# State-space stage of a two-layer hybrid block: tiles ordered by tables, head steps spread into the next group, three projection banks, normalisation moved into attention

## Chip, core and metric

The kernel runs on one core of one Trainium2 chip. A core has five engines that run their own instruction streams side by side and wait for each other by semaphores: TensorE (PE, matrix products into the eight PSUM banks `ps0` to `ps7`; the profile shows its weight loads as PEld), VectorE (DVE), ScalarE (ACT), GpSimd (POOL) and SyncE (SP, which here issues the transfers). The metric is the device time of one execution in microseconds (us), the median of three runs. The output has to agree with the reference.

## What is computed

Two layers of a first block are followed by two layers of a second one. The change touches only the first block, and in it the state-space branch. Cut to what matters (`x` is 256 tokens by 1024; 32 heads of width 64 in 4 groups of 8; state 128):

```python
for layer in range(2):
    proj = einsum('bsd,de->bse', x, w_in[layer])       # z 2048, xbc 3072, dt 64, attention inputs, gates 3072
    xbc = silu(centred_dwconv(xbc, conv_w, conv_b))    # 5 taps along the tokens
    xs, bm, cm = split(xbc)                            # 2048, 4 groups x 128, 4 groups x 128
    dt = softplus(dt_raw + dt_bias)                    # 2 directions x 32 heads
    # both directions: y[q] += sum_s (cm[q].bm[s]) * exp(cum[q] - cum[s]) * dt[s] * xs[s]
    y = y_fwd + y_bwd + d_skip * xs
    y = y * silu(z)
    y_ssd = rmsnorm(y, norm_w)                         # over all 2048 channels
    # differential attention, memory cross attention, gates
    merged = g0 * (y_ssd @ w_br_ssd) + g1 * (y_diff @ w_br_diff) + g2 * (y_cross @ w_br_cross)
    x = layernorm(ALPHA * x + merged @ w_out)
```

## The kernel before

**Weights and tiles.** Every product with a weight matrix is made in tiles of 128 output columns by 256 tokens. All are fp32, split in two: SyncE loads a unit of 256 weight columns (two tiles, 512 KB) into one of two `raw` buffers (L367); ScalarE copies a tile of it to `w_hi` (`split`, L956); VectorE makes `w_lo = raw - w_hi` (`split`, L1389); TensorE makes a tile with 24 matmuls, three for each of 8 slices (`proj` and `passes`, L498 to L500). There are four tile places in `w_hi` and `w_lo`, so TensorE may be at most four tiles behind the splits. A `raw` buffer is loaded again when both engines have split both its tiles. Each engine works in the order in which its code is written.

**State-space stage.** Each group has 16 tiles: x0 to x3, b, c (convolution inputs), z0 to z3, and six gate tiles. Their results go to two banks, `ps0` and `ps1`, by turns. ScalarE takes a tile out of its bank. A convolution tile is copied to `conv_in` and gets its first tap from ScalarE (`first_tap`), four taps from VectorE (`conv`, L1596, one `SCALAR_TENSOR_TENSOR` each), a tanh from ScalarE and its product from VectorE (`conv_silu`, L1601). When all six are through, TensorE transposes x (L655), multiplies b by c (L660), and VectorE makes `x_dt` (L1630) and the masked `cb` (L1635 to L1638). Then come the eight heads: TensorE spreads a row of cumulated decay over 128 partitions (`spread_rows`, L668), ScalarE makes the decay (`decays`, four Relu pieces and an Exp, L953), VectorE weighs it with `cb` (`weigh`, L1643), TensorE multiplies two heads at a time (`head_pair`, L681), VectorE adds the skip and applies z (`gate_y`, L1648 and L1651), ScalarE squares, GpSimd sums. The last seven tiles of the group are written between the head steps, and the heads end with the group.

**Start of a layer.** TensorE makes tiles 0 to 2 (`first_three`) and `dt_tiles` (L619 to L621). VectorE works `dt_softplus` (L1563 to L1582) behind the fourth convolution tile. `cumulate` (L630 to L637) waits for it, and the head steps wait for `row_ready`, which VectorE gives at L1623.

**Behind the stage.** TensorE sums the squares (`square_sum`, L698), VectorE makes 1/(mean + eps), ScalarE the root, and VectorE scales the 16 tiles of `y_ssd` (L1671) before it goes on to the splits of the first attention step. In attention (4 steps of 20 tiles) `token_tile` (L712 to L714) needs two of these splits at once. The branch stage begins with ScalarE's and VectorE's split of all `y` tiles (`y_hi`, `y_lo` at L1748); ScalarE waits for `ssd_ready` before the first and for `att_ready` before the third.

## Time and profile before

| | |
|---|---|
| runs, us | 2633.53, 2632.78, 2635.39 (median 2633.53) |
| the profiled execution, us | 2640.17 |
| its span (first to last instruction), us | 2638.4 |
| mean granted TensorE clock | 0.983 |
| TensorE matmul / weight load busy | 94% / 89% |
| VectorE / ScalarE busy | 65% / 51% |
| read from memory | 372.31 MB, 142 GB/s |

The state-space stage runs from about 51 to 318 us in layer 0 and from 703 to 977 us in layer 1; the attention steps follow. A row of the timeline gives the start, the time, the engine, the line and what is written and read, and in brackets how long the engine was idle before it and what ended that. Times of neighbouring instructions overlap a little, so that a cost is best read from one start to the next. Of a matmul the end is modelled; starts are what to go by.

### The profile page before, as it was taken

To read this page: it belongs to the slowest core of one execution; us is meant where nothing else is said; L and a number is where in the kernel's file an instruction comes from. 1 tells how busy PE (TensorE), PEld (TensorE's weight loads), DVE (VectorE), ACT (ScalarE), POOL (GpSimd) and SP (SyncE) were. 2 spreads that over 40 slices of the span, in tenths; PEclk is the share of its full clock that TensorE was granted. 3 is DMA by queue.
4 is the path that set the end of the run, shared out by engine and by line. 5 is a ranking of instruction groups with operands and counts; after the bars stand their busy time and mean duration, and the time that the engine had idled before them with its cause. 6 is when DMAs were issued, how large, how long until landed. Compare 5 with 4: busy or idle time off the path is not lost.

```text
span 2638.4 us, 51861 instructions
## 1 busy us (share of the span) xinstructions
PE 2470.2 (94%) x18994; PEld 2352.6 (89%) x18994; DVE 1725.0 (65%) x2597; ACT 1349.5 (51%) x2368; POOL 88.9 (3%) x96
## 2 busy tenths in 40 slices
PE   5888899999978889999999999999999999989998
PEld 4788799999978879999999998789999999779998
DVE  4677766765767776676576566567656656557655
ACT  4677644553567764555344444534445444544443
POOL 0000000000000000000010010001001001001000
PEclk9999999999989999999999999999999999999999
DMA  5344444435334444443545544234554554423553
GB/s 153 112 129 129 128 131 156 138 123 186 114 112 129 129 128 135 153 143 122 183 151 180 171 149 146 84 128 159 175 171 151 173 175 147 124 89 123 181 173 109
DMA packets 386828, 375.60 MB, mean 142 GB/s; under 512 B 14894, under 2 KB 385502, under 8 KB 386542
## 3 DMA queue, kind: packets, MB, share of 16 engines
q1 hardware_dynamic: 386670, 373.41, 44.9%
q8 instruction: 109, 1.79, 0.3%
q14 instruction: 49, 0.40, 0.0%
HBM read 372.31 MB, written 1.05 MB: 142 GB/s over the span
## 4 chain that ended last, share of the span: by engine, by line
PE 65%; issue 24%; DVE 5%; ACT 3%; POOLq 1%; DVEq 1%; DMA 1%; POOL 0%; SPq 0%; ACTq 0%
PE ps L498 18%; PE ps L500 18%; PE ps L499 18%; PE ps L712 1%; POOLq L463 1%; ACT w_hi L956 1%; PE ps L713 1%; PE ps L714 1%; DVE w_lo L1389 1%; PE ps L738 1%; PE ps L484 1%; DVE xT L1495 1%; PE ps L726 1%; PE ps L769 1%; PE ps L759 1%
## 5 line engine op out<-in xcount | busy, mean ns | idle before, releaser
L1389 DVE TENSOR_TENSOR w_lo<-raw,w_hi 128x1024 fp32r<-128x1024 f32 x704 | 860.6, 1229 | 441.7 <-ACT w_hi L956 439.5
L498 PE MATMUL ps<-x_hi,w_hi 128*128 128x272 f32 (+1 forms) x3648 | 1062.4, 291 | 24.1 <-DVE w_lo L1389 16.6
L499 PE MATMUL ps<-x_lo,w_hi 128*128 128x272 f32 (+1 forms) x3648 | 1043.2, 286 | 0.0
L500 PE MATMUL ps<-x_hi,w_lo 128*128 128x272 f32 (+1 forms) x3648 | 1042.0, 286 | 0.0
L956 ACT ACTIVATE w_hi<-raw 128x1024 fp32r<-128x1024 f32 x704 | 736.1, 1054 | 538.6 <-PE ps L500 378.0
L498 PEld LDWEIGHTS ps<-x_hi,w_hi 128*128 128x128 f32 x3648 | 690.5, 189 | 55.0 <-issue 27.6
L499 PEld LDWEIGHTS ps<-x_lo,w_hi 128*128 128x128 f32 x3648 | 692.0, 190 | 2.4
L500 PEld LDWEIGHTS ps<-x_hi,w_lo 128*128 128x128 f32 x3648 | 692.2, 190 | 0.0
L498 PE MATMUL ps<-big_r,w_hi 128*128 128x272 f32 x832 | 244.6, 294 | 12.3 <-DVE scratch L1934 8.6
L500 PE MATMUL ps<-big_r,w_lo 128*128 128x272 f32 x832 | 242.8, 292 | 0.0
L956 ACT ACTIVATE scratch<-ps 128x256 f32<-128x256 f32 (+7 forms) x312 | 115.5, 384 | 184.9 <-PE ps L714 89.8
L499 PE MATMUL ps<-gates_r,w_hi 128*128 128x272 f32 x704 | 202.4, 288 | 0.0
L499 PE MATMUL ps<-big_r,w_hi 128*128 128x256 f32 (+1 forms) x640 | 185.5, 290 | 0.0
L498 PEld LDWEIGHTS ps<-big_r,w_hi 128*128 128x128 f32 x832 | 159.3, 191 | 14.6 <-issue 14.2
L500 PEld LDWEIGHTS ps<-big_r,w_lo 128*128 128x128 f32 x832 | 159.4, 192 | 0.0
L953 ACT ACTIVATE scratch<-ps 128x272 f32<-128x272 f32 (+2 forms) x168 | 66.8, 400 | 180.1 <-PE ps L500 164.5
L498 PE MATMUL ps<-scratch_r,w_hi 128*128 128x256 f32 x512 | 146.6, 286 | 4.4 <-DVE big_r L1748 4.4
L500 PE MATMUL ps<-scratch_r,w_lo 128*128 128x256 f32 x512 | 145.7, 285 | 0.0
L499 PEld LDWEIGHTS ps<-gates_r,w_hi 128*128 128x128 f32 x704 | 132.7, 189 | 0.2
L1596 DVE SCALAR_TENSOR_TENSOR scratch<-scratch,pa_all 128x256 f32<-128x256 f32 x192 | 92.9, 484 | 53.1 <-ACT scratch L953 28.7
L499 PEld LDWEIGHTS ps<-big_r,w_hi 128*128 128x128 f32 x640 | 125.3, 196 | 0.0
L453 POOL TENSOR_TENSOR xT<-xT,norm_bias 128x272 f32<-128x272 f32 (+1 forms) x56 | 51.5, 952 | 1786.1 <-DVE x_lo L1503 1786.1
(287 smaller groups left out, 3102.8 us busy)
## 6 DMA issues: line engine op xcount, KB each, us to landing
raw<-in_w_in SPq DMA_DIRECT2D x224, 512.0 KB, 4.7
raw<-in_ffn_w_up SPq DMA_DIRECT2D x176, 512.0 KB, 4.3
raw<-in_ffn_w_down SPq DMA_DIRECT2D x64, 512.0 KB, 4.3
raw<-in_mix_w_in SPq DMA_DIRECT2D x64, 512.0 KB, 4.6
raw<-in_w_mem_kv SPq DMA_DIRECT2D x32, 512.0 KB, 4.3
raw<-in_w_br_ssd SPq DMA_DIRECT2D x32, 512.0 KB, 4.3
raw<-in_ffn_w_down SPq DMA_DIRECT2D x32, 384.0 KB, 3.5
raw<-in_w_br_diff SPq DMA_DIRECT2D x16, 512.0 KB, 4.0
```

The lines of the kernel that those rows point to most:

```text
L453: m = pool.tensor_tensor(x, x, norm_bias[:, o:o + 1].to_broadcast([P, n]), ALU.add)
L463: pool.drain()
L484: m = mm(out, w, x, start=(j == 0), stop=(j == n - 1))
L498: mm(out, wh, xh, start=first, stop=False)
L499: mm(out, wh, xl, start=False, stop=False)
L500: return mm(out, wl, xh, start=False, stop=last)
L712: mm(out, xh, wh, start=(j == 0), stop=False)
L713: mm(out, xh, wl, start=False, stop=False)
L953: return act.activation(out, in_, f, **kw)
L956: return act.activation(out, in_, ACT.Copy, scale=scale)
L1389: tt(w_lo[:, p % PARTS, :, :], raw[:, p // 2 % RAW, :, (p % 2) * P:(p % 2 + 1) * P], wh_f[:, p % PARTS, :, :], ALU.subtract).then_inc(lo_r ...
L1596: m = stt(c, conv_in[:, j, n:n + SEQ], tap(n), c, ALU.mult, ALU.add)
```

## The change

- The group loop of SyncE and the attention loops of ScalarE and VectorE are written out instead of looped. The order of the 16 tiles of a group, and the place (the tile number) behind which each head step stands, come from tables. A place of 16 or more lies in the next group (or, for the last group, in the first attention step).
- Projection tiles take three banks (`ps0`, `ps1`, `ps5`) in turn; TensorE waits for the tile three back to be taken out. Sum of squares and `cb` move to `ps7`.
- ScalarE takes the middle tap straight from the bank and `conv` makes the taps 0, 1, 3, 4. `decays` writes the Relu pieces straight to `decay`, so it waits for `y_done` before them. The z tiles no longer share a buffer with the convolution.
- The row of `row_ready` is made by VectorE at place 8 of group 0, behind five convolution tiles, and TensorE waits for it before tile 9.
- The norm: TensorE sums the squares behind tile 7 of attention step 0, ScalarE takes the root behind the root of that step, VectorE inverts at its end and scales 6, 5 and 5 tiles in steps 1, 2 and 3. `ssd_ready` is given at the end of step 3.

```diff
+CONV_ORDER = ("b", "c", "x0", "x1", "x2", "x3")
+FIRST_GROUP = ("g0", "g1", "z0", "z1", "b", "c", "x0", "x1", "x2", "x3", "g2", "g3", "z2", "z3", "g4", "g5")
+NEXT_GROUP = ("b", "c", "x0", "x1", "g0", "g1", "x2", "x3", "z0", "z1", "g2", "g3", "z2", "z3", "g4", "g5")
+SPREAD_AT = later((9, 10, 11, 12, 15, 16, 17, 18), (3, 4, 6, 7, 13, 14, 15, 16))
+DECAY_AT = later((10, 11, 12, 13, 16, 17, 18, 19), (4, 5, 8, 9, 14, 15, 16, 17))
+WEIGH_AT = later((11, 12, 13, 14, 17, 18, 19, 20), (7, 8, 10, 11, 15, 16, 17, 18))
+PAIR_AT = later((15, 16, 19, 21), (13, 14, 17, 19))
+GATE_AT = later((16, 17, 20, 22), (14, 15, 18, 20))
+CB_AT, MASK_AT = later(9, 5), later(10, 6)
+XS_AT, XDT_AT = later(13, 11), later(14, 12)
+NORM_TILES = ((), range(0, 6), range(6, 11), range(11, 16))
...
 # TensorE
+                    for k in range(16):
+                        n = g * 16 + k
+                        if n >= 3:
+                            pe.wait_ge(gf[(n - 3) % 2], LH + A_H + (n - 3) // 2 + 2)
+                            proj(Q, T, k, k, x1, own=banks[(n + 1) % 3])
+                        if n == 6:
+                            cumulate()
+                        if n == 8:
+                            pe.wait_ge(S["cum_ready"], l + 1)
+                            pe.wait_ge(S["row_ready"], l + 1)
+                            pe.wait_ge(S["rows_cleared"], l + 1)
+                        if g:
+                            heads(g - 1, k + 16)
+                        heads(g, k)
...
 # VectorE
+                    for k in range(16):
+                        if MASK_AT[g] == k:
+                            mask_cb(g)
+                        if XDT_AT[g] == k:
+                            x_by_dt(g)
+                        if tiles[k] in CONV_ORDER:
+                            conv(CONV_ORDER.index(tiles[k]), k)
+                        if g == 0 and k == 2:
+                            dt_exponent()
+                        split(Q, k + 4)
+                        if tiles[k][0] == "z":
+                            z_silu_tile(int(tiles[k][1]), k)
+                        if k >= 3 and tiles[k - 3] in CONV_ORDER:
+                            conv_silu(CONV_ORDER.index(tiles[k - 3]))
+                        if g == 0 and k == 3:
+                            dt_softplus()
+                        if g == 0 and k == 8:
...
+                        if g:
+                            heads(g - 1, k + 16)
+                        heads(g, k)
...
-                v.wait_ge(S["ssq_done"], l + 1)
-                ts(rs_ssd[:, 0, :], ps[5][:, 0:SEQ], 1.0 / SSD_INNER, NORM_EPS, ALU.mult, ALU.add)
-                v.drain()
-                v.reciprocal(rs_ssd[:, 1, :], rs_ssd[:, 0, :]).then_inc(S["ssd_var"], 1)
...
+                    for j in NORM_TILES[i]:
+                        norm_y(j)
...
+                    if i == 0:
+                        v.wait_ge(S["ssd_rs"], l + 1)
+                        v.reciprocal(rs_ssd[:, 0, :], rs_ssd[:, 1, :])
+                    if i == 3:
+                        v.drain()
+                        v.sem_inc(S["ssd_ready"], 1)
```

Three places where instructions move, all on VectorE, each with the semaphores waited for. First, the start of a layer. Before, `dt_softplus` (from `waits dt_exp`) stands behind convolution taps:

```order
L1596 SCALAR_TENSOR_TENSOR scratch<-scratch,pa_all 128x256
L1596 ISA
L1596 SCALAR_TENSOR_TENSOR scratch<-scratch,pa_all 128x256
L1388 REGISTER_ALU
L1389 TENSOR_TENSOR w_lo<-raw,w_hi 128x1024 [waits weights_hi_ready]
L1601 SCALAR_TENSOR_TENSOR scratch<-scratch 128x256 [waits conv_tanh]
L1561 REGISTER_ALU
L1563 TENSOR_SCALAR big<-big 128x128 [waits dt_exp]
```

After, it stands behind two splits and the two z tiles (`bank_free`), and no tap has been made yet:

```order
L1630 SCALAR_TENSOR_TENSOR big<-big 128x128
L1461 REGISTER_ALU
L1462 TENSOR_TENSOR w_lo<-raw,w_hi 128x1024 [waits weights_hi_ready]
L1442 ISA
L1727 SCALAR_TENSOR_TENSOR scratch<-scratch 128x256 [waits bank_free0]
L1461 REGISTER_ALU
L1462 TENSOR_TENSOR w_lo<-raw,w_hi 128x1024 [waits weights_hi_ready]
L1727 SCALAR_TENSOR_TENSOR scratch<-scratch 128x256 [waits bank_free1]
L1634 REGISTER_ALU
L1636 TENSOR_SCALAR big<-big 128x128 [waits dt_exp]
```

Five convolution tiles now stand between the softplus and the row for `row_ready`, where before there were two.

Second, a head of a middle group. Before, `weigh` (L1643) stands between a split and `gate_y`, with no taps near:

```order
L1389 TENSOR_TENSOR w_lo<-raw,w_hi 128x1024
L1642 REGISTER_ALU
L1643 TENSOR_TENSOR big<-big,scratch 128x768
L1388 REGISTER_ALU
L1389 TENSOR_TENSOR w_lo<-raw,w_hi 128x1024
L1648 ISA
L1648 SCALAR_TENSOR_TENSOR scratch<-scratch,skip,ps 128x256
L1651 SCALAR_TENSOR_TENSOR big<-scratch 128x256
```

After, places 16 to 18 of a group: each `weigh` (now L1682) stands behind the four taps (L1714) and the split of a convolution tile of the next group:

```order
L1714 SCALAR_TENSOR_TENSOR scratch<-scratch,pa_all 128x256
L1461 REGISTER_ALU
L1462 TENSOR_TENSOR w_lo<-raw,w_hi 128x1024 [waits weights_hi_ready]
L1681 REGISTER_ALU
L1682 TENSOR_TENSOR big<-big,scratch 128x768 [waits decay_ready]
L1442 REGISTER_ALU
L1714 ISA [waits bank_free0]
L1714 SCALAR_TENSOR_TENSOR scratch<-scratch,pa_all 128x256
```

The head pair that waits for this `weigh` now waits for those taps as well.

Third, the entry of attention. Before, the norm (a loop of four times four `L1671`) stands ahead of the first splits:

```order
L1664 TENSOR_SCALAR scratch<-ps 128x256 [waits ssq_done]
L1666 RECIPROCAL scratch<-scratch 128x256
L1667 UNCONDITIONAL_BRANCH
L1671 ISA [waits ssd_rs]
L1671 ISA
L1671 SCALAR_TENSOR_TENSOR big<-big,pb_all,scratch 128x256
```

After, the splits of attention step 0 stand between the last three `weigh` and two `gate_y` of the last group:

```order
L1462 TENSOR_TENSOR w_lo<-raw,w_hi 128x1024 [waits weights_hi_ready]
L1681 REGISTER_ALU
L1682 TENSOR_TENSOR big<-big,scratch 128x768 [waits decay_ready]
L1461 REGISTER_ALU
L1462 TENSOR_TENSOR w_lo<-raw,w_hi 128x1024 [waits weights_hi_ready]
L1681 REGISTER_ALU
L1682 TENSOR_TENSOR big<-big,scratch 128x768 [waits decay_ready]
L1688 ISA [waits y_done]
```

The norm is gone from here, and with it the wait for `ssq_done`.

## Rows read from the trace of the kernel before

**Rows 1.** The page, section 1: engine, busy us (share), instructions.

```profile
PE 2470.2 (94%) x18994; PEld 2352.6 (89%) x18994; DVE 1725.0 (65%) x2597; ACT 1349.5 (51%) x2368; POOL 88.9 (3%) x96
```

**Rows 2.** Waits of PE, whole run: who waited, for whom, total us, times, longest.

```profile
PE ps L681 <- DVE big L1643: 22.0, 14, 2.7
PE ps L498 <- DVE w_lo L1389: 16.6, 11, 6.9
PE ps L655 <- issue: 11.4, 2, 5.8
...
PE ps L712 <- DVE w_lo L1389: 6.5, 2, 3.3
```

**Rows 3.** Windows: one group in each layer, then attention entry (stretch, length, busy, PEclk).

```profile
218.00:282.20 64.20, 56.64 (x469) 52.68 (x469) 47.84 (x75) 46.29 (x94) 4.49 (x4) 1.00 0.44 132
875.30:941.10 65.80, 58.34 (x469) 53.91 (x469) 47.93 (x75) 46.27 (x94) 4.49 (x4) 0.97 0.42 129
318.30:346.10 27.80, 22.69 (x156) 21.71 (x155) 19.13 (x35) 8.02 (x13) 1.46 (x2) 0.88 0.36 114
```

**Rows 4.** Timeline of PE: a tile starts, a spread row and a pair, the next tile.

```profile
98.66 0.28 PE L498 MATMUL ps<-x_hi,w_hi 128*128 128x256 f32 x1
...
101.50 0.40 PE L668 MATMUL ps<-cum_rows,head_sel 128*128 128x512 f32 x1
...
103.28 0.38 PE L498 MATMUL ps<-x_hi,w_hi 128*128 128x256 f32 x1
```

**Rows 5.** Timeline of DVE: a convolution tile, its split, a product; a later split.

```profile
208.63 0.48 DVE L1596 SCALAR_TENSOR_TENSOR scratch<-scratch,pa_all 128x256 f32<-128x256 f32 x1
...
210.99 1.22 DVE L1389 TENSOR_TENSOR w_lo<-raw,w_hi 128x1024 fp32r<-128x1024 f32 x1
212.12 0.42 DVE L1601 SCALAR_TENSOR_TENSOR scratch<-scratch 128x256 f32<-128x256 f32 x1
...
214.82 1.22 DVE L1389 TENSOR_TENSOR w_lo<-raw,w_hi 128x1024 fp32r<-128x1024 f32 x1
```

**Rows 6.** Timeline of DVE: x_dt (cb follows), a weigh; then a gate_y.

```profile
224.32 2.48 DVE L1630 TENSOR_TENSOR scratch<-ps,dt_tok 128x512 f32<-128x512 f32 x4
...
228.02 0.96 DVE L1643 TENSOR_TENSOR big<-big,scratch 128x768 f32<-128x768 f32 x1 [0.16 <-issue]
...
237.93 0.48 DVE L1648 SCALAR_TENSOR_TENSOR scratch<-scratch,skip,ps 128x256 f32<-128x256 f32 x1 [0.21 <-issue]
...
238.83 0.95 DVE L1643 TENSOR_TENSOR big<-big,scratch 128x768 f32<-128x768 f32 x1
```

**Rows 7.** Timeline of ACT: a split that waited for its transfer, then a head's decay and the next.

```profile
221.76 1.06 ACT L956 ACTIVATE w_hi<-raw 128x1024 fp32r<-128x1024 f32 x1 [4.31 <-DMA raw<-in_w_in]
222.72 1.34 ACT L953 ACTIVATE scratch<-ps,cum_tok 128x256 f32<-128x256 f32 x4
...
224.89 1.33 ACT L953 ACTIVATE scratch<-ps,cum_tok 128x256 f32<-128x256 f32 x4
```

**Rows 8.** Timeline of DVE, layer 1: softplus's first, the tap behind it, the row.

```profile
724.22 0.22 DVE L1563 TENSOR_SCALAR big<-big 128x128 f32<-128x128 f32 x1
...
730.38 0.48 DVE L1596 SCALAR_TENSOR_TENSOR scratch<-scratch,pa_all 128x256 f32<-128x256 f32 x1
...
746.19 0.68 DVE L1623 TENSOR_TENSOR cum_rows<-ps,cum_rows 32x512 fp32r<-32x512 f32 x1
```

**Rows 9.** Attention entry: the norm on DVE, ahead of the splits.

```profile
326.79 6.42 DVE L1671 SCALAR_TENSOR_TENSOR big<-big,pb_all,scratch 128x256 f32 x16 [0.81 <-ACT scratch L953]
```

**Rows 10.** Start of the branch stage: ACT's first copies, DVE's first `y_lo`.

```profile
562.33 1.99 ACT L956 ACTIVATE scratch_r<-big 128x1024 fp32r<-128x1024 f32 x2
...
565.20 6.90 DVE L1748 TENSOR_TENSOR big_r<-big,scratch_r 128x1024 fp32r<-128x1024 f32 x6 [0.18 <-issue]
```

**Rows 11.** Windows in which the granted clock was at its lower level.

```profile
335.00:341.80 6.80, 5.74 (x26) 5.65 (x27) 3.28 (x3) 0.21 (x1) 0.00 (x0) 0.50 0.69 226
823.10:826.50 3.40, 3.40 (x18) 2.95 (x15) 3.08 (x5) 2.66 (x6) 0.00 (x0) 0.50 0.53 138
```

More of the change, by code:

```diff
@@ L73 @@
 K_EPS = K_INV + 1
-K_SUB = K_EPS + 2
+K_SUB = K_EPS + 3
 K_COLS = K_SUB + P
@@ new lines, in heads @@
+                def heads(g, at):
+                    for j in range(HEADS_PER_GROUP):
+                        if SPREAD_AT[g][j] == at:
+                            spread_rows(g, j)
+                    for p in range(4):
+                        if PAIR_AT[g][p] == at:
+                            head_pair(g, p)
+                    if XS_AT[g] == at:
+                        turn_x(g)
+                    if CB_AT[g] == at:
+                        b_by_c(g)
+                banks = (ps[0], ps[1], ps[5])
@@ new lines, in square_y, with heads @@
+                def square_y(g, p):
+                    n = g * 4 + p
+                    act.wait_ge(S["y_gated"], l * 16 + n + 1)
+                    if n >= 2:
+                        act.wait_ge(S["sq_added"], l * 16 + n - 1)
+                    fn(y_sq[:, p % 2, :], y_ssd[:, n, :], ACT.Square).then_inc(S["y_squared"], 1)
+                def heads(g, at):
+                    for j in range(HEADS_PER_GROUP):
+                        if DECAY_AT[g][j] == at:
+                            decays(g, j)
+                    for p in range(4):
+                        if SQUARE_AT[g][p] == at:
+                            square_y(g, p)
@@ L1056, in _ @@
-                    copy(conv_in[:, :, 0:2], zeros)
-                    copy(conv_in[:, :, 2 + SEQ:4 + SEQ], zeros)
-                    for j in range(6):
-                        done(T, j)
-                        bank = {2: ps[6], 3: ps[5]}.get(j, ps[j % 2]) if g == 0 else ps[j % 2]
-                        copy(conv_in[:, j, 2:2 + SEQ], bank[:, 0:SEQ]).then_inc(gf[j % 2], 1)
-                        act.drain()
-                        first = g * 4 + j if j < 4 else g + 16 + 4 * (j - 4)
-                        fn(xbc[:, j, :], conv_in[:, j, 0:SEQ], ACT.Identity, scale=taps[:, ds(l * PA_ROWS + first, 1)],
-                           bias=pb_[:, ds(l * PB_ROWS + first + PB_CONVB, 1)]).then_inc(S["first_tap"], 1)
-                        split(Q, j + 4)
-                        if j:
-                            conv_tanh(j - 1)
-                        if g == 0 and j == 2:
+                    tiles = GROUP_TILES[g]
@@ new lines, in conv_first @@
+                    def conv_first(c, k, b):
+                        if g and c >= 2:
+                            act.wait_ge(S["y_gated"], G * 4 + c - 5)
+                        first = g * 4 + c - 2 if c >= 2 else g + 16 + 4 * c
+                        out = x_c[:, c - 2, :] if c >= 2 else bc[:, c, :]
+                        fn(out, b, ACT.Identity, scale=taps[:, ds(l * PA_ROWS + first + 2 * CONV_TILES, 1)],
+                           bias=pb_[:, ds(l * PB_ROWS + first + PB_CONVB, 1)])
+                        copy(conv_in[:, c, 2:2 + SEQ], b).then_inc(gf[k % 2], 1)
@@ new lines, in _ @@
+                    if g == 0:
+                        zeros = view(const, K_CAUS2, 6, 2)
+                        copy(conv_in[:, :, 0:2], zeros)
+                        copy(conv_in[:, :, 2 + SEQ:4 + SEQ], zeros)
+                        for k in range(3):
+                            evac_tile(k)
+                    for k in range(16):
+                        if g or k >= 3:
+                            evac_tile(k)
+                        split(Q, k + 4)
+                        if k >= 2 and tiles[k - 2] in CONV_ORDER:
+                            conv_tanh(CONV_ORDER.index(tiles[k - 2]))
+                        if g == 0 and k == 2:
@@ L1134, in _ @@
+                        if g:
+                            heads(g - 1, k + 16)
+                        heads(g, k)
+                for i in range(4):
                     Q, T, N = L + i * 4 + B_Q, LH + i * 8 + B_H, l * 4 + i
@@ L1676, in _, with norm_y @@
+                def norm_y(j):
+                    y = y_ssd[:, j, :]
+                    stt(y, y, pb_[:, ds(l * PB_ROWS + (PB_NORM + j), 1)], rs_ssd[:, 0, :], ALU.mult, ALU.mult)
+                for i in range(4):
                     Q, T, N = L + i * 4 + B_Q, LH + i * 8 + B_H, l * 4 + i
```

387 lines of the change are left out of this document (187 added, 200 removed).

## Prediction

> **What bounds the kernel now.** I read the page first: TensorE is busy 94% of the span and VectorE 65% [rows 1], so time is lost only where TensorE waits. The list of its waits says for whom: nearly all of the long ones end with VectorE's work (`weigh` at L1643, `w_lo` at L1389), and the wait at L655 is the start of a layer [rows 2]. The windows then tell where. A group in the middle of the state-space stage takes 64.2 us in layer 0, of which TensorE is busy 56.6 and VectorE 47.8, and 65.8 in layer 1, where the granted clock has also been at its lower level (1.2 instead of 2.4 GHz) for one stretch; the entry of attention takes 27.8 us with 22.7 busy [rows 3]. So about 7.6 us in each middle group, 5 at each attention entry and some 10 to 14 at each layer start are waits. All this is some 90 us, half of it within the groups.
>
> **Prices.** TensorE: a tile 98.66 to 101.50 = 2.84; spread row and pair together 1.78, of which I give the row 0.34 [rows 4]. VectorE: four taps 2.36, a split 1.13, a product with the tanh about 0.34 (0.42 less the overlap) [rows 5]; `x_dt` and masked `cb` together 3.7, `weigh` 0.88 (0.96 less the overlap), `gate_y` 1.1 with the idle ahead of it [rows 6]. ScalarE: split 0.96, a head's decay 2.17 [rows 7]; taking out a tile 0.3 to 0.8. A transfer into a `raw` buffer is usable 5.7 us after VectorE's last split of it: the one that starts at 214.82 ends at 216.0 [rows 5], and ScalarE's split that waits for the transfer starts at 221.76 [rows 7]. The work of TensorE stays the same but for its place. So the sum is one of waits, and I worked a timetable, place for place, each engine in its new order, with these prices.
>
> **The start of a layer.** Before, `row_ready` comes at 746.9 in layer 1 [rows 8]. After, VectorE sits idle until z1 is out of its bank (about 717.9, since tile 3 ends behind the dt tiles), works the softplus of 724.22 to 730.38 = 6.2 [rows 8] until 724.1, and then five convolution tiles with splits (5 x 3.5), two products and the row: 18.9, so `row_ready` comes at 743.0. TensorE has done tile 8 at 732.5 and waits 10.5 in one piece for it, where before it waited 6.9 for a `w_lo` and 5.8 for the row [rows 2]. Behind it the transposes wait 1.3 for the product of x3. Counting what head work is still owed at the end of the group's 16 tiles, layer 1 gains 3.6 us; in layer 0, where ScalarE was not late before, the same timetable gives 0.1. Sum **-4**.
>
> **Groups 1 to 3.** In places 0 to 2 VectorE now makes four taps, a split, and behind them a `weigh` or `gate_y` of the group before: 4.4 to 5.5 us a place, against 2.84 to 4.6 on TensorE. The pair at place 17 needs the `weigh` of place 16, which comes 5.7 us after tile 0 is done, while TensorE is there after 3.2: wait 2.5. The pair at 19 waits 2.4 in the same way. Then the transposes at place 11 wait for the product of x3, which stands behind split 14. That split waits for a transfer released by split 11, behind x3's own taps: 5.7 + 0.96 + 1.13 + 0.34 = 8.2 us after it, wait 2.3. Group 1 is worse, because group 0's tables are later by two places: 4.3, 0.5 and 3.4. In all 22.6 by starts (about 20.8 as the windows count idle), against three times 7.6: a gain of 2.0 a layer, 4 in both. So the waits do not leave the groups, they change their place. The clock of before fell once within a group in layer 0 and three times in layer 1 (823.10 is one of them) at some 1.6 each [rows 11]: 6.5 comes back if it stays up. Sum **-10.5** before what the clock does after the change.
>
> **Attention entry.** The norm (6.4 us of VectorE [rows 9] ahead of four splits) goes, and with it the wait of `token_tile`, the wait for the square sum and the lower clock from 335.0 to 341.8 [rows 11]. The stretch of 27.8 [rows 3] holds 19.0 of work at full clock (four tiles, two token tiles of 2.9, 1.8 for the rotation); the pairs moved into it are owed by the groups. VectorE has only 1.13 + 0.88 a place here, so its pairs wait 0.4 each. 0.35 of the square sum is only moved. 27.8 - 19.0 - 0.8 - 0.35 = 7.65 a layer: **-15.3**. This is the surest term.
>
> **The norm's new place.** 16 products of 0.40 [rows 9] in three steps stand on VectorE ahead of a split that ScalarE had ready some 4 us before TensorE needs it, and 1.75 for the inversion stands ahead of splits which end 1.3 us before their token tile: zero. If the cover were gone, the queue behind them (splits 4 and 5 of step 1) would cost at most 1.75 a layer. ScalarE's root costs nothing, it stands next to another root.
>
> **The branch stage.** `ssd_ready` now comes at the end of step 3. ScalarE's first two copies, at 562.33, move behind VectorE's last product: the first `y_lo`, at 565.20 [rows 10], comes when one copy is through, 1.05 later. Sum **+2.1**.
>
> **Loops written out.** TensorE waits for nothing at the loop ends of attention, so 0; bounds: -2 and +4, the latter from the idle of some 2.6 that ScalarE shows once around a table load at the start of layer 1.
>
> **The clock after the change.** Sum so far: -4 - 10.5 - 15.3 + 2.1 = -27.7. Eight waits of over 2 us are left in groups 1 to 3 of a layer, 16 in all. The rows show both outcomes of such waits: after the 2.7 us at a head pair [rows 2] the clock stayed up in two of three groups of layer 0 (1.00 in rows 3), in layer 1 it fell each time, for 3.4 us at 0.50 (823.10), and around the 3.3 us at the token tile [rows 2] it was down for 6.8 (335.00) [rows 11]. A fall costs half of what of it is worked: 1.7 or 2.9. For the two long waits of group 1 I take 2.3 each, for the six others every second time 1.7: 9.7 a layer, of which about a fifth falls into the next wait anyway. That is +16. The Trainium skill ("TensorE: Matmul & The Clock Gate", section "Why this matters for your kernels") warns of idle gaps between bursts of matmuls, since the clock then drops. By that rule, with which the falls in the trace agree, splitting the waits into more pieces does not help unless each gets short; taken strictly it gives the slower rival below.
>
> **Sum.** -27.7 + 16 = -11.7. From the profiled execution, 2640.2, this is 2628.5; the runs' median lies 6.6 lower at 2633.5, so I forecast **2622**.
>
> **Rivals.**
> 1. *The clock stays up.* All 16 waits pass without a fall, since TensorE works at least two tiles between them. For it speaks layer 0, against it layer 1. -27.7: **2606**. If VectorE also lags less than by my timetable (its sum of 52 us a group fits under 56), the three waits of a group shrink by 1 us each, 18 more: 2588 is the far end.
> 2. *The clock falls after every one of the 16 waits and takes 6.8 us to come back*, as it did at 335.00 [rows 11]: 16 x 2.9 = 46 against 27.7: +18, **2652**, slower. It decides from 27.7 / 16 = 1.7 us a wait on. Against it: waits of 2.7 us so far cost 1.6 or nothing.
> 3. *Gain and loss cancel.* ScalarE now has decays, tanh and two passes of a convolution tile in one place (2.2 + 0.3 + 0.8 + 0.96 = 4.3 against 2.84), so a split reaches VectorE late, and what VectorE does late meets TensorE as a longer wait. 2 us more in each of six groups is 12: **2633.5**, no change.
> 4. *The change doesn't take effect*: the norm is in fact gone from the entry by the order of instructions, so this could only hold for the groups, and there it is my forecast that they gain 2 us a layer.
>
> **How the numbers follow.** Forecast 0.48, rival 1 0.17, rival 2 0.18, rival 3 0.17. The measurement tells some 0.2%, 5.3 us, from no change. Faster: forecast and rival 1, less the forecast's own upper tail, 0.62; the same 0.16; slower 0.22. The forecast's own range is 2610 to 2630. The range of 8 in 10 takes in most of rival 1 and rival 2 short of its last third: 2601 to 2646.
>
> **What would show it.** In the changed profile: one wait of about 10.5 us of TensorE for the row at the start of each layer; per group, waits of about 2.5, 2.4 and 2.3 us for `weigh`, `weigh` and a product of the convolution, longer in group 1; an attention entry with no wait over 1 us and a full clock; the branch stage's first wait 1 us longer than before. Middle groups of 63 us at full clock would be the forecast, under 60 rival 1's far end, over 65 rival 2 or 3, told apart by the granted clock. The forecast is wrong if VectorE's places 0 to 3 take other than 4.4 to 5.5 us, or if the transfer is not what gates x3's product.

## The result, and the profile after

The changed kernel takes **2667.5 us** (median of 4 runs, 2665.4 to 2672.0) against 2633.2 us for the kernel before (4 runs, 2629.3 to 2635.4): ratio 1.0131, 95% interval 1.0119 to 1.0143. It is slower by 34 us, where I had forecast 2622 us and a range that ended at 2646. The profiled execution took 2672.0 us with a span of 2670.2, which is 31.8 us more than the span of before.

The page of the changed kernel, section 1, answers to [rows 1]: engine, busy us, share of the span, instructions.

```profile
PE 2483.3 (93%) x18994; PEld 2365.7 (89%) x18994; DVE 1730.0 (65%) x2595; ACT 1335.5 (50%) x2354; POOL 82.1 (3%) x96
```

TensorE has the same 18994 matmuls and is 13 us longer busy with them. More matmul time for the same matmuls goes with a lower clock: the mean granted clock of the profiled execution is 0.973, where it was 0.983. The list of TensorE's waits answers to [rows 2] (who waited, for whom, total us, times, longest). L703 is the head pair (L681 before), L673 the transposes of x (L655 before), L524 the first matmul of a projection tile (L498 before):

```profile
PE ps L703 <- DVE big L1682: 44.7, 16, 5.5
PE ps L673 <- DVE scratch L1722: 26.2, 8, 5.3
PE ps L524 <- issue: 20.5, 2, 10.3
```

The pairs' waits for `weigh` have doubled, from 22.0 to 44.7 us. A wait of 26.2 us for the product with the tanh (`conv_silu`) has taken the place of 11.4 us in which the transposes waited at the layer starts. The two waits of 10.3 are the row at the start of a layer, and they are as long as forecast. The long waits for `w_lo` inside the stage and the wait at the token tile (L712 before) are gone. ("issue" stands where the profile shows no engine that TensorE waited for.)

Windows of the changed kernel, from the first matmul of a group's first tile to that of the next group's: group 1, 2 and 3 of layer 0, the same of layer 1, then the stretch from attention's first tile to the rotation in each layer. Columns: stretch, length, busy (instructions) of PE, PEld, DVE, ACT and POOL, granted clock, DMA share, GB/s. The rows for group 2 and the entry answer to [rows 3]. Group 1 has 5.3 us of group 0's head steps in it.

```profile
119.00:193.20 74.20, 62.40 (x488) 57.33 (x487) 50.20 (x77) 45.40 (x95) 3.44 (x4) 0.91 0.38 114
193.20:262.50 69.30, 59.51 (x469) 55.39 (x468) 49.29 (x74) 44.88 (x92) 3.60 (x4) 0.95 0.40 122
262.50:334.00 71.50, 60.77 (x469) 56.39 (x468) 49.30 (x74) 44.91 (x92) 3.60 (x4) 0.93 0.38 119
790.70:865.50 74.80, 62.79 (x488) 57.67 (x487) 50.23 (x77) 45.45 (x95) 3.44 (x4) 0.91 0.37 113
865.50:935.10 69.60, 59.45 (x470) 55.34 (x469) 49.30 (x74) 44.91 (x92) 3.60 (x4) 0.95 0.40 122
935.10:1009.10 74.00, 62.80 (x470) 57.92 (x468) 49.29 (x74) 44.91 (x92) 3.60 (x4) 0.88 0.37 115
334.00:354.00 20.00, 17.97 (x154) 16.52 (x153) 12.50 (x15) 13.83 (x28) 2.67 (x3) 1.00 0.36 114
1009.10:1029.10 20.00, 17.97 (x155) 16.55 (x154) 12.50 (x15) 13.83 (x28) 2.68 (x3) 1.00 0.37 117
```

A group takes 69 to 75 us where it took 64 to 66, the granted clock is at 0.88 to 0.95 instead of 1.00 or 0.97, and VectorE is busy for 49 of the 70. It is not short of time over a group as a whole. The entry of attention is the one place that went as planned: full clock and hardly a wait.

Cut at the first matmuls of the same tiles, both layers together, the 31.8 us are these. In the second line the work that the change moves over a border is put back to where it was: 5.3 us a layer of head steps from group 0 into group 1, and 3.2 us a layer from group 3 into attention (three pairs and three spread rows, then two pairs and one row; a row 0.34, a pair 1.44, [rows 4]).

| Stretch | layer start and group 0 | groups 1 to 3 | entry to the rotation | steps of attention | branch stage to next start | the rest |
|---|---|---|---|---|---|---|
| after less before, us | -11.1 | +42.4 | -6.1 | +0.2 | +4.1 | +2.3 |
| moved work put back | -0.5 | +38.2 | -12.5 | +0.2 | +4.1 | +2.3 |
| forecast | -4 | +5.5 (-10.5 +16) | -15.3 | 0 | +2.1 | 0 |

So 32.7 of the 43.5 us between the forecast for the profiled execution (2628.5) and what it took lie in groups 1 to 3.

**One wait, read out.** Four timelines of the changed kernel around the pair of place 17 in layer 0 (start, us, engine, line, what, and in brackets the idle time ahead with what ended it). TensorE first: the last matmul of tile 0, then the pair.

```profile
265.24 0.27 PE L526 MATMUL ps<-x_hi,w_lo 128*128 128x256 f32 x1
...
272.62 2.81 PE L703 MATMUL ps<-big,scratch 128*64 128x256 f32 x16 [3.97 <-DVE big L1682]
```

ScalarE, which takes tile 0 out at L1001 and L1004 (266.39 and 266.84):

```profile
263.90 1.35 ACT L1001 ACTIVATE big<-ps,cum_tok 128x256 f32<-128x256 f32 x4
265.33 0.85 ACT L1001 ACTIVATE big<-big 128x768 f32<-128x768 f32 x1
266.08 0.40 ACT L1001 ACTIVATE y_sq<-big 128x256 f32<-128x256 f32 x1
266.39 0.55 ACT L1001 ACTIVATE scratch<-ps,pb_all,pa_all 128x256 f32<-128x256 f32 x1
266.84 0.37 ACT L1004 ACTIVATE scratch<-ps 128x256 f32<-128x256 f32 x1
```

VectorE and, in the last row, GpSimd: a `weigh`, the two instructions of the gating, the first tap of tile 0, its split, the `weigh` that releases the pair, and GpSimd's addition to the sum of squares.

```profile
265.18 0.95 DVE L1682 TENSOR_TENSOR big<-big,scratch 128x768 f32<-128x768 f32 x1
266.35 0.48 DVE L1688 SCALAR_TENSOR_TENSOR scratch<-scratch,skip,ps 128x256 f32<-128x256 f32 x1 [0.21 <-issue]
266.90 0.68 DVE L1691 SCALAR_TENSOR_TENSOR big<-scratch 128x256 f32<-128x256 f32 x1
267.50 0.47 DVE L1714 SCALAR_TENSOR_TENSOR scratch<-scratch,pa_all 128x256 f32<-128x256 f32 x1
...
269.86 1.22 DVE L1462 TENSOR_TENSOR w_lo<-raw,w_hi 128x1024 fp32r<-128x1024 f32 x1
271.00 1.48 DVE L1682 TENSOR_TENSOR big<-big,scratch 128x768 f32<-128x768 f32 x1
...
270.70 0.96 POOL L491 TENSOR_TENSOR y_sum<-y_sum,y_sq 128x256 f32<-128x256 f32 x1 [3.41 <-ACT y_sq L1001]
```

My timetable had this `weigh` ready 5.7 us after tile 0 was done, and it took 7.0 (265.5 to 272.48). Two things were missing in it. When tile 0 ends, ScalarE still has place 15's decay and square to do, and VectorE the `weigh` and the gating of place 15 (until 267.58). ScalarE has tile 0 out at 267.21, so of the two it is VectorE's own queue that ends last. So the first tap starts 2.0 us after the tile, where my 5.7 leaves 1.3 once four taps, a split and a `weigh` are taken off. And the `weigh` takes 1.48 us where I had 0.88. These 1.3 us make up most of the 1.8 between the wait forecast (2.5, from start to start) and the gap measured (4.26); most of the rest is that TensorE was there 2.9 us after tile 0 and not 3.2.

### The profile page after: what moved, and what is told of

The parts are those of the page before. It is cut to its first block, busy times and chain, and to the rows that moved or that the text cites. A ratio compares the mean times of both kernels' runs of the same rounds, so it can differ in the third digit from the quotient of the medians.

```text
span 2670.2 us, 51795 instructions
## 1 busy us (share of the span) xinstructions
PE 2483.3 (93%) x18994; PEld 2365.7 (89%) x18994; DVE 1730.0 (65%) x2595; ACT 1335.5 (50%) x2354; POOL 82.1 (3%) x96
## 3 DMA queue, kind: packets, MB, share of 16 engines
HBM read 372.31 MB, written 1.05 MB: 140 GB/s over the span
## 4 chain that ended last, share of the span: by engine, by line
PE 76%; DVE 9%; ACT 5%; issue 3%; DVEq 3%; DMA 3%; ACTq 1%; SPq 0%
PE ps L524 20%; PE ps L526 20%; PE ps L525 20%; ACT w_hi L1004 2%; DVE w_lo L1462 2%; PE ps L703 2%; DVE scratch L1714 1%; PE ps L757 1%; PE ps L758 1%; PE ps L759 1%; ACT big L1001 1%; DVEq L1686 1%; DMA raw<-in_w_in 1%; ACTq L1106 1%; ACT scratch L1004 1%
## 5 line engine op out<-in xcount | busy, mean ns | idle before, releaser
L524 PE MATMUL ps<-x_hi,w_hi 128*128 128x272 f32 (+1 forms) x3648 | 1066.2, 292 | 28.9 <-issue 20.5
L1004 ACT ACTIVATE w_hi<-raw 128x1024 fp32r<-128x1024 f32 x704 | 736.4, 1055 | 493.0 <-PE ps L526 375.6
L524 PEld LDWEIGHTS ps<-x_hi,w_hi 128*128 128x128 f32 x3648 | 696.2, 191 | 54.5 <-issue 45.2
L524 PE MATMUL ps<-big_r,w_hi 128*128 128x272 f32 x832 | 244.9, 294 | 12.8 <-DVE scratch L2030 9.1
L1004 ACT ACTIVATE scratch<-ps 128x256 f32<-128x256 f32 (+7 forms) x312 | 116.0, 386 | 218.4 <-PE ps L526 115.4
L524 PEld LDWEIGHTS ps<-big_r,w_hi 128*128 128x128 f32 x832 | 159.7, 192 | 14.9 <-issue 14.5
L1001 ACT ACTIVATE scratch<-ps 128x272 f32<-128x272 f32 (+2 forms) x168 | 66.9, 401 | 179.9 <-PE ps L526 164.7
L524 PE MATMUL ps<-scratch_r,w_hi 128*128 128x256 f32 x512 | 146.3, 286 | 5.7 <-DVE big_r L1844 5.7
L1714 DVE SCALAR_TENSOR_TENSOR scratch<-scratch,pa_all 128x256 f32<-128x256 f32 x192 | 96.2, 501 | 66.8 <-ACT scratch L1004 41.0
```

The costliest lines, as they stand in the source:

```text
L524: mm(out, wh, xh, start=first, stop=False)
L1001: return act.activation(out, in_, f, **kw)
L1004: return act.activation(out, in_, ACT.Copy, scale=scale)
L1714: m = stt(out, conv_in[:, c, n:n + SEQ], taps[:, ds(l * PA_ROWS + first + n * CONV_TILES, 1)], out, ALU.mult, ALU.add)
```

## The experiments

Each run is told against the kernel before on the same chip. "Gap" is the time between the starts of two neighbouring matmuls of TensorE, as my forecast counted waits.

**1. The norm part alone.** The kernel before with the norm moved into attention, as the change has it, and attention's loops written out; the group loop as it was.

```diff
-                        if i == k == 0:
-                            square_sum()
...
                     proj(Q, T, 7, 7, x1)
+                    if i == 0:
+                        square_sum()
...
+                    for j in NORM_TILES[i]:
+                        norm_y(j)
```

> The kernel before with one part of the change alone: the norm of the state-space output moved out of the entry of attention (sum of squares by TensorE behind tile 7 of step 0, root on ScalarE next to another root, inversion on VectorE at the end of step 0, the 16 products in steps 1 to 3) and attention's four steps written out; the group loop, its order, its two banks and the head steps stay as before. My terms for this part were -15.3 (two attention entries of 7.65) and +2.1 (branch stage), with 0 for the new place and for written-out loops: 2633 - 13 = 2620, ratio 0.995, and the fall of the clock at the entry (335.0 in layer 0, 993.7 in layer 1) should be gone. Theory A (the loss of the changed kernel comes wholly from the group part): this kernel is faster than before, 2616 to 2624. Rival B (the norm part or the written-out loops lose time too, for instance by products ahead of the splits in attention): 2633 or more.

Measured: **2619.8 us**, ratio 0.9943 (0.9925 to 0.9961). Attention's entry in its trace (from the first tile to the rotation, layer 0):

```profile
319.46:333.87 14.41, 14.41 (x123) 14.38 (x122) 7.71 (x9) 6.05 (x10) 1.48 (x2) 1.00 0.47 147
```

TensorE is busy for the whole stretch at full clock. In the kernel before the same stretch took 23.0 (318.35 to 341.35): 8.6 gained, where the forecast had 7.65. Theory A holds: this part is worth what the sum said (-13.2 forecast, -14 measured), and the whole loss of 34, in fact 48 against this kernel, comes with the rest of the change, the new order of the groups and the layer start.

**2. The pairs a place later.**

```diff
-PAIR_AT = later((15, 16, 19, 21), (13, 14, 17, 19))
+PAIR_AT = ((15, 16, 20, 21), (13, 14, 18, 20), (13, 14, 18, 20), (13, 14, 17, 19))
```

(`GATE_AT` and `SQUARE_AT` of these pairs are moved with them, by one place.)

> The changed kernel, but the head pairs 2 and 3 of a group, with their gating and squares, stand one place later in the next group (places 18 and 20 instead of 17 and 19 for groups 1 and 2; 20 and 21 instead of 19 and 21 for group 0; group 3 as it was). Nothing else is moved. In the changed kernel TensorE waits 4.3 and 3.2 us for them. Theory L (latency: the weighted decay comes 5.7 to 7 us after tile 0, and only the place is too early): both waits go, at least for groups 1 and 2, some 5 us a group less, four such groups and the clock falls with them: -20 to -30 against the changed kernel, 2638 to 2648. Theory W (work: VectorE has more to do in places 0 to 10 than TensorE, so the time is owed anyway): the wait of the transposes for the product of x3 grows by what the pairs lose; within 6 us of the changed kernel, 2662 to 2673.

Measured: **2647.5 us**, ratio 1.0049 (1.0030 to 1.0067), 20 us faster than the changed kernel. The gaps of 4.26 and 3.18 at these pairs became 1.4 and 1.3 to 1.6, that of 5.8 at group 0's last pairs 2.4; TensorE's idle time ahead of all pairs fell from 44.7 to 19.7 us. The transposes of group 3 in layer 0 now waited longer, as the row shows (3.71 in the changed kernel):

```profile
309.19 0.47 PE L673 MATMUL ps<-const,scratch 128*128 128x128 f32 x1 [4.61 <-DVE scratch L1722]
```

and a gap of 2.5 at the product of b and c (place 5) of groups 2 and 3 was new. So part of it moved on, as theory W says, but most was gone: theory L.

**3. The product ahead of the split.**

```diff
+                        if g and k >= 3 and tiles[k - 3] in CONV_ORDER:
+                            conv_silu(CONV_ORDER.index(tiles[k - 3]))
                         split(Q, k + 4)
```

> The changed kernel, but in groups 1 to 3 VectorE makes the product with the tanh of a convolution tile ahead of the split of its place instead of behind it. In the changed kernel the split at place 10 of group 3 starts at 314.27 because its transfer is late, and the product of x3 behind it ends at 315.8, while its tanh was there at 309.8 and TensorE was at the transposes at 312.4. Theory T (the transfer gates the transposes, as the prediction has it): the wait of 3 to 5 us at the transposes falls to below 1.5 in six groups, -2.5 x 6 = -15, with the clock falls that hang on it up to -25: 2642 to 2652. Rival V (VectorE is late by its own work, the taps): the wait stays and the time too, 2662 to 2670.

Measured: **2647.5 us**, ratio 1.0052 (1.0033 to 1.0072), again 20 us faster. The chain that it cuts, in the changed kernel, place 10 of group 3: ScalarE's split that waits for its transfer, VectorE's split behind it, the product of x3, the transposes.

```profile
313.18 1.06 ACT L1004 ACTIVATE w_hi<-raw 128x1024 fp32r<-128x1024 f32 x1 [0.83 <-DMA raw<-in_w_in]
...
314.27 1.23 DVE L1462 TENSOR_TENSOR w_lo<-raw,w_hi 128x1024 fp32r<-128x1024 f32 x1 [1.93 <-ACT w_hi L1004]
315.41 0.42 DVE L1722 SCALAR_TENSOR_TENSOR scratch<-scratch 128x256 f32<-128x256 f32 x1
...
316.14 0.41 PE L673 MATMUL ps<-const,scratch 128*128 128x128 f32 x1 [3.71 <-DVE scratch L1722]
```

And the transposes in the run with the product ahead:

```profile
306.80 0.33 PE L673 MATMUL ps<-const,scratch 128*128 128x128 f32 x1 [0.85 <-DVE scratch L1722]
```

The idle time ahead of the transposes fell from 26.2 to 9.7 us over all eight. The edit moves the product of every convolution tile of groups 1 to 3 (six a group, 36 in all, each 0.42 us) ahead of the split of its place, and nothing else; that it is x3's that counts is read from the rows. The transfer is the one forecast: VectorE's split 11, which frees the buffer, ended at 307.32, and ScalarE could start at 313.18, 5.9 us later for the 5.7 forecast. Theory T.

**4. The clock kept up.** Everything waits as in the changed kernel, but TensorE works matmuls without a reader while it would be idle.

```diff
+                def warm(n, count):
+                    if count:
+                        pe.wait_ge(gf[(n - 2) % 2], LH + A_H + (n - 2) // 2 + 2)
+                        for j in range(count):
+                            mm(banks[(n + 2) % 3][:, 0:SEQ], mem_hi[:, j % KT, 0:P], mem_hi[:, j % KT, :], start=True, stop=True)
...
+WARM_AT = {8: 84, 19: 42, 21: 8, 27: 38, 33: 30, 35: 22, 43: 22, 49: 30, 51: 22, 59: 30}
```

> The changed kernel with matmuls added whose result nobody reads, in TensorE's queue ahead of the waits: 84 ahead of the row at the layer start, 42 and 8 ahead of group 0's last pairs, 30 and 22 ahead of the pairs of groups 1 and 2, 38, 22 and 30 ahead of the transposes of groups 1 to 3; at 0.12 us each they are a little shorter than the waits. No wait of another engine is changed. In the groups of the changed kernel the clock is at its lower level for 35 us in layer 0 and 43 in layer 1, and TensorE worked nearly all of it, which cost some 34 us; before it was 7. Theory C (the clock is half of the loss): the falls go, and the time with them by as much as the work and not the other engines' pace set the end: -15 to -30, 2638 to 2653. Rival P (VectorE and ScalarE set the pace and TensorE at full clock only waits longer): within 5 of the changed kernel, 2662 to 2673.

Measured: **2636.6 us**, ratio 1.0009 (0.9999 to 1.0019), 31 us faster than the changed kernel. Group 2 of either layer:

```profile
187.90:254.20 66.30, 65.26 (x544) 61.61 (x543) 49.30 (x74) 44.92 (x92) 3.60 (x4) 1.00 0.42 128
843.20:909.60 66.40, 65.29 (x544) 61.64 (x543) 49.31 (x74) 44.91 (x92) 3.62 (x4) 1.00 0.42 128
```

The clock does not fall once in the groups. They take 407.5 us in both layers together, against 433.4 in the changed kernel and 391.1 before, so the clock cost **26 us** there. In the changed kernel the clock was down in these groups for 31 us in layer 0 and 38 in layer 1. TensorE did not work through all of it, as the expectation has it, but for 54.5 us, as the sum over the fourteen stretches at the lower clock shows (their length, and TensorE's busy time in them):

```profile
sum 68.27, PE 54.47; mean PE 3.89
```

Half of that is 27, and 26 came back. Theory C. What is left against before is the waits themselves: 407.5 less the 4.2 us of head steps that are moved into groups 1 to 3 (10.6 in, 6.4 out) is 12.2 more than 391.1, in which the clock was down for 13.7.

**5. Both orders together.** Edits 2 and 3, no added matmuls.

> The changed kernel with both edits of the two runs before it: pairs 2 and 3 a place later (for groups 0 to 2) and the product with the tanh ahead of the split (groups 1 to 3). Each alone took 20 us off. In the first, the transposes still waited 3 to 5.8 us; in the second, the pairs still waited 4.2 and 3.2. Theory S (two separate causes, the order of VectorE's queue at two places): the gains add up, less the clock falls that both counted, 2622 to 2634. Rival W (one shortage of VectorE behind both, which the first edit only pushed to the other place): the sum falls short by more than half of the second gain, 2638 to 2648.

Measured: **2619.2 us**, ratio 0.9943 (0.9926 to 0.9959). That is 48 us faster than the changed kernel, where the two apart took 40 off. The 8 us more are within the uncertainty of the four times, so what is shown is that the gains add up, as theory S has it; the time is just under its range. The windows of group 2:

```profile
189.30:251.20 61.90, 56.39 (x469) 52.79 (x468) 48.67 (x74) 45.03 (x92) 4.23 (x4) 1.00 0.46 137
834.30:896.50 62.20, 56.46 (x469) 52.83 (x468) 48.67 (x74) 45.04 (x92) 4.22 (x4) 1.00 0.46 136
```

With either edit alone one kind of long wait was left and the clock still fell in this group (0.90 to 0.97 granted). With both, no gap in groups 1 to 3 is over 2.7 us, and in group 2 the clock stays at 1.00. Group 2 is at 62 us, 2 to 4 under the kernel before, so rival W is out. But 2619.2 is also the time of run 1 (2619.8), which has the norm part alone: with these two orders the new groups lose nothing against the old ones and gain nothing over the whole kernel. What groups 2 and 3 win goes in part to the two head pairs that now stand in attention's entry (17.0 us from the first tile to the token tile against 11.5 in run 1, of which 3.2 is their own work).

**6. The softplus a place earlier.**

```diff
-                        if g == 0 and k == 3:
+                        if g == 0 and k == 2:
                             dt_softplus()
```

> The changed kernel, but in group 0 VectorE works the softplus of dt one place earlier, behind the product of place 2, where it sits idle for 4.9 us for ScalarE's split (in the run with the added matmuls from 714.2 to 719.1; the exponential it needs ends at 713.1), and not behind place 3. Theory Q (the wait of 10.5 us for the row at each layer start is the length of VectorE's queue from the softplus on): the row comes some 5 us earlier, the wait falls to 5 to 6, two layers: -10, with the clock falls there up to -14, 2653 to 2659. Rival D (the row waits for transfers or for ScalarE, or the following waits take it back): less than 4 us, 2663 or more.

Measured: **2660.4 us**, ratio 1.0102 (1.0086 to 1.0119), 7 us faster, less than theory Q had it. The gap at the row fell from 10.5 to 7.3, not to 5 or 6. In layer 1 the softplus starts 18.1 us after the layer's first matmul (in run 4, which has the old place, 24.6), but the row comes only 4.2 earlier: the split and the product of place 3, which VectorE used to have done before, now stand behind the softplus (1.5), and once it waits 0.7 for a tile. The queue is the cause, the size was not read closely enough.

**7. All three orders with the clock kept up.** The three edits, and added matmuls at the waits that are left.

> The changed kernel with pairs 2 and 3 later, the product ahead of the split, the softplus earlier, and matmuls whose result nobody reads ahead of the waits then left (40 ahead of the row, 12 ahead of group 0's last pair, 14 ahead of the transposes of group 1, 10 ahead of the product of b and c in groups 2 and 3). If all four causes are separate as my theory has it, -20 -20 -12 and some -10 for the clock that is still lost: 2595 to 2610, below both kernels. Rival (VectorE's total work, about 52 of 56 us a group, stops the gain): a group settles at 62 us or more and the time at 2615 or more.

Measured: **2604.5 us**, ratio **0.9885** (0.9868 to 0.9902), the fastest kernel here. Group 2 stays at 62 us, which was the rival's sign, but the time is 10 us under the rival's: the rest of the gain lies at the layer start, in group 1 and in the clock.

**8. The norm part with the clock kept up in the old group order.**

> The kernel before with the norm part of the change (2619.8 in its run) and matmuls whose result nobody reads ahead of three waits of the old group order: 38 ahead of the row at the layer start, and in groups 1 to 3 10 ahead of the product of b and c and 20 ahead of the first pair. The clock fell at these waits for 6.8 us at each layer start and for 3.4 in four groups; TensorE worked 6 and 3.4 of it. Theory C: 3 a layer and 1.7 a fall come back, -10 to -13: 2607 to 2610. Rival P (the other engines set the pace there): 2615 to 2621.

Measured: **2617.8 us**, ratio 0.9932 (0.9913 to 0.9951). Against run 1 (0.9943) that is within the intervals: rival P, or no effect to be told. Of the four falls within groups in run 1 three are still there, in layer 1 some 9 us earlier in the kernel (at 805.4 and 870.2 instead of 814.3 and 879.1), though its start is only 2 us earlier; at the row the clock was down for 3.4 us instead of 6.8 in layer 0, and not at all in layer 1, where the fall ahead of it grew from 3.4 to 6.8. Since the falls did not go away, this run does not say what the clock costs the old order.

**9. The squares later.**

```diff
-SQUARE_AT = later((17, 18, 21, 23), (15, 16, 19, 21))
+SQUARE_AT = later((17, 21, 21, 23), (15, 19, 19, 21))
```

> The changed kernel, but ScalarE squares the second pair of heads (and GpSimd adds it) some three places later: places 19 instead of 16 in groups 1 to 3, 21 instead of 18 in group 0. In the trace of the changed kernel six weightings on VectorE take 1.48 to 1.50 us where the other 58 take 0.95, and each of the six runs beside an addition on GpSimd (270.70 to 271.66 beside 271.00 to 272.48); two in each layer's groups stand right ahead of the pair at place 17. Theory G (the two slow each other down when they run at once): no weighting of 1.5 us is left at place 16, the wait at the pair of place 17 falls from 4.26 to about 3.4 (0.53, and the square's 0.3 off ScalarE's queue ahead of tile 0), four such waits and one each in group 1, so -3 to -6, 2661 to 2665. Rival N (the long weightings have another cause): they stay, and the time within 2 us of 2667.

Measured: **2670.8 us**, ratio 1.0146 (1.0131 to 1.0162); no gain. The rows say what theory G said: the four long weightings at place 16 are gone, two at another place are left, and the gap at the pair is 3.72 instead of 4.26. That is the 0.53 of the `weigh` alone. The square that was moved stood behind tile 0's work in ScalarE's queue (at 270.23 in the changed kernel), and not ahead of it as the expectation has it; the one ahead, at 266.08, is that of the first pair and stayed. So this run does not test what ScalarE's queue costs.

```profile
274.49 0.95 DVE L1682 TENSOR_TENSOR big<-big,scratch 128x768 f32<-128x768 f32 x1
...
275.58 0.65 PE L703 MATMUL ps<-big,scratch 128*64 128x256 f32 x4 [3.45 <-DVE big L1682]
```

In the traced execution the clock took the gain back. Windows of group 2, to be read against 69.3 and 69.6 us at 0.95:

```profile
194.60:266.00 71.40, 62.00 (x469) 57.44 (x468) 48.72 (x74) 44.84 (x92) 3.36 (x4) 0.90 0.40 119
864.00:935.70 71.70, 62.18 (x470) 57.50 (x469) 48.75 (x74) 44.84 (x92) 3.36 (x4) 0.90 0.40 118
```

The group waits half a microsecond less and is two longer, since the clock was down for 13.7 us in it instead of 6.8. How much of that is the edit's doing is not shown: in run 6, whose groups have the order of the changed kernel, group 2 of layer 1 took 71.0 and group 3 of layer 0 73.9, where the changed kernel has 69.6 and 71.5.

**10. The three orders without added matmuls.**

> The changed kernel with the three edits of order (pairs 2 and 3 later, the product ahead of the split, the softplus earlier) and no added matmuls. With the two first it took 2619; the softplus alone took 7 off; with all three and the added matmuls it took 2604.5. If the softplus brings its 7 here too, 2610 to 2614, and the added matmuls of the earlier run were worth 6 to 9. If the added matmuls carried nothing, 2602 to 2607. If the softplus brings nothing without them, 2617 to 2621.

Measured: **2612.0 us**, ratio 0.9919 (0.9905 to 0.9932). The softplus brings its 7 here too, and the added matmuls of run 7 were worth another 7.5, as expected.

**11. Pairs a further place later.** Run 7 with pairs 2 and 3 of groups 1 and 2 at places 19 and 21.

> The kernel of three orders with added matmuls, with pairs 2 and 3 of groups 1 and 2 a further place later (19 and 21), the square of their first pairs at places 15 and 19, and the added matmuls set to the waits left (54 ahead of the row, 12, 14, 12, 14 ahead of group 0's last pair and the transposes of groups 1 to 3). What waits of 1.4 and 1.6 us were left at places 18 and 20 should go: -2.5 in four groups and some of the clock, 2592 to 2600. Rival: the wait moves on to the transposes, whose product comes from VectorE: 2602 to 2607.

Measured: **2607.2 us**, ratio 0.9905 (0.9892 to 0.9919), not told apart from run 7. The waits at places 18 and 20 went, and one of 2.2 to 2.5 us is there at the product of b and c (place 5), where run 7 has ten added matmuls and this run none. The rival's outcome, though the wait moved on to another step than it named.

## Why the prediction was wrong, point by point

- **Attention's entry (-15.3):** right. Alone (run 1) it gave 8.6 a layer against 7.65. In the changed kernel it gave 12.5 in both layers together, since the two pairs moved into it waited 1.6 and 1.0 and not 0.4 each.
- **The norm's new place (0):** right, +0.2. **Loops written out (0):** no sign of a cost; run 1 has them and meets the sum.
- **Branch stage (+2.1):** small, +4.1, but not as forecast (1.05 a layer): 3.7 in layer 0 and 0.4 in layer 1. The first wait there is 3.1 against 2.5, and in layer 0 the clock stayed down for 6.8 us behind it instead of 3.4.
- **Layer start (-4):** the wait of 10.5 in one piece was right to 0.1, and 1.4 at the transposes too. The sum came to -0.5: 0.0 in layer 0, where 0.1 was forecast, and 0.6 in layer 1, where it was 3.6. In layer 1 the softplus began 24.8 us after the layer's first matmul and not 23.1, and the row came 1.7 later too; why, and where the rest went, no run shows. The clock was down for 10 to 14 us around that wait, as it was before for about as long in two pieces.
- **The waits of groups 1 to 3 (-4): the first step that failed.** The places were right; the sizes were not. By gaps I had 22.6 us a layer and the trace has 34.3 and 35.3, so +24 in both layers: the pair at 17 waited 4.26 for 2.5, that at 19 3.18 for 2.4, the last pairs of group 0 5.8 and 1.3 for 4.3 and 0.5, the transposes 5.4 to 5.6, 3.0 to 3.4 and 4.0 to 4.4 for 3.4, 2.3 and 2.3. I started each place when its tile was done. In the trace VectorE, and ScalarE a little less, still owe work of the place before at that moment (0.7 us of the pair at 17), and an addition on GpSimd made the `weigh` 0.5 longer. The sign that I had set for this step does not catch it: VectorE's places 0 to 2 took 4.9, 4.4 and 5.6 us in group 3 of layer 0, for 4.4 to 5.5. The work of a place was right; when it began was not. That the waits could be longer than by the timetable was rival 3, for 2 us a group; it was about 4. That the order at these places is the cause, and not a lack of VectorE's time, is shown by runs 2, 3 and 5.
- **The clock (+16): the second step.** It cost 26 in the groups (run 4). I had let half of the six waits of over 2 us outside group 1 pass without a fall and priced a fall at 1.7, and those of group 1 at 2.3. Nearly each wait was longer than forecast, and of the eight of over 2 us in each layer seven have a fall beside them, of 6.8 us instead of 3.4 in two cases in layer 0 and in four in layer 1: 31 and 38 us in all. What the prediction quoted from the Trainium skill ("TensorE: Matmul & The Clock Gate", section "Why this matters for your kernels"), that idle gaps between bursts of matmuls lower the clock, is borne out by run 4: with matmuls in the gaps the clock did not fall in the groups. The two steps are not separate: a longer wait costs once as idle and once more as a slow stretch behind it.
- **The rivals:** I had "the clock falls after every wait" (2652) and "ScalarE and VectorE are late" (2633.5) as exclusive cases, each worked out with the other at its forecast. They came together, and they feed each other. Both at once, 2652 + 12 = 2664, lay outside the range.
- **Transfer and product of x3:** the chain was right (run 3). In group 3 of layer 0 it took 8.5 us from the end of split 11 to the end of the product, for 8.2. The wait grew from 2.3 to 3.98 mainly because TensorE was there 4.8 us after that split and not 5.9: the split itself was late against TensorE.

By the forecast's own sum: 2628.5 for the profiled execution, +32.7 in the groups (by run 4, 12.2 for -10.5 before the clock and 26 for 16 from the clock), +3.5 start, +2.8 entry, +2.0 branch and +2.5 elsewhere gives 2672.0.

## What to carry to other kernels

When steps of one stage are spread into the next, work the timetable of every engine in the chain at the seam, not only of the one that ends it: what an engine still owes at that moment is easily left out (0.7 us at one pair here, and the waits of a group came out some 4 us too short in all). Ask for each in-order queue what stands ahead of the one short instruction that TensorE waits for: here moving products of 0.42 us ahead of the splits beside them, and two pairs by one place, turned a loss of 34 us into a gain of 14. Ask also what that gain is made of: the norm part alone gave the same 14, so with these two orders the spread head steps only cease to cost time, and it took the softplus and the added matmuls to get below that. Where waits of some microseconds are left between the matmuls, cost them together with the clock, as one risk; a cheap test is to fill them with matmuls that nobody reads, though in the old order (run 8) three of four falls in the groups stayed.

## What was not expected of the hardware

- Of 64 weightings on VectorE, 58 take 0.95 us and six 1.48 to 1.50, and each of the six runs beside an addition of two buffers on GpSimd (in one case 270.70 to 271.66 on GpSimd, 271.00 to 272.48 on VectorE). The addition also shows 0.96 there against 0.74 alone. When run 9 moved the addition, the four at that place were 0.95 again. The Trainium skill ("SBUF — State Buffer", section "SBUF: two separate sides") says that VectorE and GpSimd share a pair of ports, which whichever starts first holds for its whole instruction if VectorE has two SBUF inputs. The trace agrees: what VectorE loses, 0.53, is about what GpSimd's addition had left to run, 0.66 by its shown end and 0.44 by its usual length. It is not the weightings alone: beside an addition a product with the tanh took 0.97 instead of 0.42 (at 226.55) and a tap 0.98 instead of 0.48 (at 285.93).
- Less waiting need not save time. Run 9 took 0.5 us of waiting out at each of four pairs, and its groups 1 to 3 of both layers took 436.8 us with the clock down for 82, against 433.5 with 68 in the changed kernel. That less waiting costs time is not shown by this: run 6, with the order of the changed kernel in these groups, took 435.6 with 68, and each number is from one execution. What is shown is that the half microsecond brought nothing. Run 5 took more out, and the clock stayed up in group 2. Between the two nothing in the trace tells in advance on which side a group will fall, and this stays open.
